# Order of the last expert stages, order of the ring's loads, and the output in parts, in a two-layer decoder on one core

## The reference, cut to what matters

```python
logits = (xf @ router_w).astype(jnp.float32) + router_b.astype(jnp.float32)
top_logit, top_e = lax.top_k(logits, TOP_K)
top_w = jax.nn.softmax(top_logit, axis=-1)
...
return (jax.nn.silu(xb @ wg[e]) * (xb @ wu[e])) @ wd[e]
...
x = x + g2 * f
```

## Time and profile before

| | |
|---|---|
| median of 3 executions | 1541.88 us (1541.83 to 1543.37) |
| profiled execution | 1549.82 us |
| its span, first to last instruction | 1547.9 us |
| PE busy | 1437.8 us (93%) |
| DVE, ACT busy | 473.4 us, 197.7 us |
| granted TensorE clock, mean | 0.984 |
| DMA, mean over the span | 311 GB/s |
| the expert layer | about 680 to 1548 us |

### The profile page before, as it was taken

How to read it: one execution, slowest core, us unless ns; L and a number is a source line. 1 busy time by engine, 2 the same in 40 slices (tenths; PEclk the granted TensorE clock), 3 DMA queues, 4 the chain that set the end, 5 groups by cost and what they waited for, 6 DMA issues and landing times.

```text
span 1547.9 us, 17255 instructions
## 1 busy us (share of the span) xinstructions
PE 1437.8 (93%) x6928; PEld 703.4 (45%) x6928; DVE 473.4 (31%) x949; ACT 197.7 (13%) x427; POOL 3.4 (0%) x32
## 2 busy tenths in 40 slices
PE   6899899999999999989777898999999999999897
PEld 2576655555544757653222333434234434343332
DVE  4478735345333565352100011101101221100103
ACT  1123223000003142321000000000001000000000
POOL 0000000000000000000000000000000000000000
PEclk9999889999999999979999999999999999999999
DMA  9945525886875333149999999999999999999995
GB/s 344 362 150 210 184 96 203 266 310 232 309 278 184 110 110 109 55 162 355 416 411 401 414 412 412 416 412 416 409 411 399 413 412 416 410 415 413 405 403 204
DMA packets 161218, 481.64 MB, mean 311 GB/s; under 512 B 18504, under 2 KB 36296, under 8 KB 146800
## 3 DMA queue, kind: packets, MB, share of 16 engines
q1 hardware_dynamic: 159688, 478.65, 80.4%
q10 hardware_dynamic: 1448, 1.84, 0.4%
HBM read 479.41 MB, written 1.06 MB: 310 GB/s over the span
## 4 chain that ended last, share of the span: by engine, by line
PE 74%; DMA 15%; DVE 5%; SPq 3%; ACT 1%; issue 1%; DVEq 0%; ACTq 0%
PE bank L1638 22%; PE bank L1674 13%; PE bank L1512 10%; DMA ring<-in_moe_wu 9%; PE bank L1234 6%; PE bank L1530 5%; PE bank L1476 4%; DMA ring<-in_moe_wg 3%; PE bank L1223 2%; DMA ring<-in_moe_wd 2%; DMA ring<-in_ada_w 1%; SPq L817 1%; PE bank L1577 1%; SPq L812 1%; DVE ada_acc L1776 1%; PE bank L1692 1%
## 5 line engine op out<-in xcount | busy, mean ns | idle before, releaser
L1638 PE MATMUL bank<-ring,h_T 128*32 128x512 f32 (+1 forms) x2240 | 300.9, 594 | 46.1 <-DMA ring<-in_moe_wu 36.1
L1674 PE MATMUL bank<-ring,m_qk_T 128*32 128x512 f32 (+2 forms) x1344 | 246.8, 594 | 14.8 <-DMA ring<-in_moe_wd 14.0
L1638 PEld LDWEIGHTS bank<-ring,h_T 128*32 128x32 f32 (+1 forms) x2240 | 92.1, 115 | 238.0 <-issue 236.4
L1638 PE MATMUL bank<-ring,cmp_region 128*128 128x512 f32 x448 | 196.3, 592 | 0.0
L1674 PEld LDWEIGHTS bank<-ring,m_qk_T 128*32 128x32 f32 (+2 forms) x1344 | 87.4, 127 | 169.8 <-issue 168.6
L1512 PE MATMUL bank<-ring,h_T 128*128 128x384 f32 (+1 forms) x448 | 156.8, 503 | 0.7 <-DVE m_s_region L2171 0.7
L1638 PEld LDWEIGHTS bank<-ring,cmp_region 128*128 128x128 f32 x448 | 84.0, 190 | 100.3 <-issue 100.3
L1234 PE MATMUL bank<-ring,h_T 128*128 128x512 f32 (+1 forms) x320 | 116.1, 512 | 0.8 <-ACT wide L923 0.5
L1512 PEld LDWEIGHTS bank<-ring,h_T 128*128 128x128 f32 x448 | 83.2, 190 | 61.3 <-issue 15.5
L2370 DVE SCALAR_TENSOR_TENSOR m_s_region<-m_s_region,bank 128x512 f32<-128x512 f32 x35 | 24.1, 688 | 255.8 <-PE bank L1638 255.8
L1069 ACT ACTIVATE m_qk_T<-bank 128x512 f32<-128x512 f32 x35 | 20.9, 597 | 637.0 <-PE bank L1654 636.3
(11 more groups left out here) (353 smaller groups left out, 1016.7 us busy)
## 6 DMA issues: line engine op xcount, KB each, us to landing
ring<-in_moe_wg SPq DMA_DIRECT2D x112, 1024.0 KB, 20.9
ring<-in_moe_wu SPq DMA_DIRECT2D x112, 1024.0 KB, 18.4
ring<-in_moe_wd SPq DMA_DIRECT2D x112, 1024.0 KB, 19.8
ring<-in_ada_w SPq DMA_DIRECT2D x28, 1024.0 KB, 8.8
ring<-in_ada_w SPq DMA_DIRECT2D x10, 2048.0 KB, 14.2
ring<-in_w_in SPq DMA_DIRECT2D x10, 2048.0 KB, 10.7
ring<-in_ffn_wg SPq DMA_DIRECT2D x6, 1536.0 KB, 10.5
ring<-in_ffn_wu SPq DMA_DIRECT2D x6, 1536.0 KB, 8.9
```

Source lines behind the costliest of these rows:

```text
L1638: last = mm(b[c0:c1, :], xT[st.team % 2][:, k, c0:c1], w, start=k == 0, stop=k == KC - 1)
L1674: last = mm(ps[half][c0:c1, :], hbT[:, unit, 128 * f + c0:128 * f + c1], w[:, D * (f % 2) + 512 * half:D * (f % 2) + 512 * half + 512], st ...
```

## The change

Four things. The last two stages of team 3 are put next to each other, and behind them those of team 4, so that stages 16 to 19 are (team 3, third span), (team 3, fourth), (team 4, third), (team 4, fourth). Team 3's four scatters go to stage 19's own hooks (`RETURN_IN[19]`): after the first and the second step of the gate part, after the up part, and after the down of stage 18. The known loads ahead of `order_ready` are ten: the eight of before and the first two of stage 1's gate part for expert 7. And the half slot of each load is chosen by `_assign`: load n goes where the load lies that PE uses up first of the 14 held, and waits for that one. The output is issued in four transfers of 128 rows of 2 KB, each as soon as its own addition is counted, ahead of the reading of the overflow count.

```diff
 for _teams in ((0,), (1, 2), (3, 4)):
-    for _s in range(len(SPANS)):
-        for _t in _teams:
-            STAGES.append(Stage(_t, _s, sum(st.units for st in STAGES)))
+    _order = [(_t, _s) for _s in range(len(SPANS)) for _t in _teams]
+    if _teams[-1] == len(TEAMS) - 1:
+        _order[-3:-1] = _order[-2], _order[-3]
+    for _t, _s in _order:
+        STAGES.append(Stage(_t, _s, sum(st.units for st in STAGES)))
...
-RETURN_IN = {5: 0, 12: 1, 13: 2}
+RETURN_IN = {5: 0, 12: 1, 13: 2, 19: 3}
...
+STEPS = []
+for _j in range(len(STAGES) + 1):
+    if _j < len(STAGES):
+        STEPS.append(("up", _j))
+    if _j:
+        STEPS.append(("down", _j - 1))
+EARLY = ((0, 0, 0), (0, 0, 1), (0, 1, 0), (0, 1, 1), (1, 0, 0))
...
-    for part in range(2):
-        for piece in range(STAGES[0].units):
-            add(STAGES[0], part, piece, (0,))
...
+    for s, part, piece in EARLY:
+        add(STAGES[s], part, piece, (0,))
+    for what, j in STEPS:
+        for part in (0, 1) if what == "up" else (2,):
+            for piece in range(STAGES[j].units):
+                add(STAGES[j], part, piece, STAGES[j].members)
...
+KNOWN = 2 * len(EARLY)
...
+def _assign():
+
+    turn = {}
+    for what, j in STEPS:
+        st = STAGES[j]
+        for part in (0, 1) if what == "up" else (2,):
+            for i in range(2 * st.units):
+                for m in st.members:
+                    turn[st.load[(part,) + divmod(i, 2) + (m,)]] = len(turn)
+    holds = list(range(SUB))
+    slot, nth, left = list(range(SUB)), [1] * SUB, [None] * SUB
+    for n in range(SUB, len(MOE_LOADS)):
+        s = min(range(SUB), key=lambda s: turn[holds[s]])
+        assert turn[holds[s]] < turn[n]
+        slot.append(s)
+        nth.append(nth[holds[s]] + 1)
+        left.append(MOE_LOADS[holds[s]][:4])
+        holds[s] = n
+    return slot, nth, left
...
-                    sub_used(sp, *MOE_LOADS[n - SUB][:4])
+                    sub_used(sp, *SUB_LEFT[n])
...
+            for n in range(2 * TT):
+                half, tt = divmod(n, 2)
+                sp.wait_ge(moe["added"], 4 * (len(TEAMS) - 1) + n + 1)
+                sp.dma_start(out[0, tt * 128:tt * 128 + 128, 512 * half:512 * half + 512], x[:, tt, 512 * half:512 * half + 512]).then_inc(out_saved, 16)
...
-            sp.wait_ge(x_final, 2 * TT)
-            for tt in range(TT):
-                sp.dma_start(out[0, tt * 128:tt * 128 + 128, :], x[:, tt, :]).then_inc(out_saved, 16)
-            sp.wait_ge(out_saved, 16 * TT)
...
+            sp.wait_ge(out_saved, 16 * 2 * TT)
...
-                        if st is STAGES[-1] and q:
-                            for n in range(4):
-                                moe_scatter(st.team - 1, n, (7, 2, 3, 4)[n])
...
-            for n in range(4):
-                add_team(len(TEAMS) - 2, n, (7, 2, 3, 4)[n])
```

More of the change, by code:

```diff
@@ L387, in _list_uses @@
+    for what, j in STEPS:
+        for part in (0, 1) if what == "up" else (2,):
+            for piece in range(STAGES[j].units):
+                add(STAGES[j], part, piece, STAGES[j].members)
 def _list_uses():
     n = 0
[L390 to L398, removed]
+    for what, j in STEPS:
+        st = STAGES[j]
+        for part in (0, 1) if what == "up" else (2,):
+            for i in range(2 * st.units - (part < 2)):
@@ L399, in _list_uses @@
                 n += 1
-                STAGES[j - 1].used[(2,) + divmod(i, 2)] = n
+                st.used[(part,) + divmod(i, 2)] = n
 _list_loads()
 _list_uses()
-assert len(MOE_LOADS) == 2 * LOADS * N_EXP and len(MOE_LOADS) % SUB == 0
-KNOWN = sum(_m == 0 for _st, _part, _, _, _m in MOE_LOADS if _st is STAGES[0] and _part < 2)
-assert all(_st is STAGES[0] and _m == 0 for _st, _, _, _, _m in MOE_LOADS[:KNOWN])
+assert len(MOE_LOADS) == 2 * LOADS * N_EXP
+KNOWN = 2 * len(EARLY)
+assert all(_st.team == 0 and _m == 0 for _st, _, _, _, _m in MOE_LOADS[:KNOWN])
@@ L410 @@
+SUB_OF, SUB_LOAD, SUB_LEFT = _assign()
 class Ordered:
@@ L679, in big_slot @@
         def big_slot(n):
-            return (n % SUB // 2 + 1) % RING
+            return (SUB_OF[n] // 2 + 1) % RING
         def moe_part(st, part, piece, q, m):
             n = st.load[part, piece, q, m]
-            return ring[:, big_slot(n), 2048 * (n % 2):2048 * (n % 2) + 2048]
+            return ring[:, big_slot(n), 2048 * (SUB_OF[n] % 2):2048 * (SUB_OF[n] % 2) + 2048]
         def moe_loaded(eng, st, part, piece, q):
@@ L691, in moe_loaded @@
                 n = st.load[part, piece, q, m]
-                eng.wait_ge(moe_full[n % SUB], 16 * (n // SUB + 1))
+                eng.wait_ge(moe_full[SUB_OF[n]], 16 * SUB_LOAD[n])
         def sub_used(eng, st, part, piece, q):
@@ L811, in _ @@
                     src = w[f0:f0 + 512, :].rearrange("(p f) n -> p (f n)", f=4)[:, 2048 * q:2048 * q + 2048]
-                    sp.dma_start(moe_part(st, part, piece, q, m), src).then_inc(moe_full[n % SUB], 16)
+                    sp.dma_start(moe_part(st, part, piece, q, m), src).then_inc(moe_full[SUB_OF[n]], 16)
                 else:
@@ L816, in _ @@
                     dst = moe_part(st, part, piece, q, m).rearrange("p (k n) -> p k n", n=c)
-                    sp.dma_start(dst, rows.rearrange("(k p) n -> p k n", p=128)).then_inc(moe_full[n % SUB], 16)
+                    sp.dma_start(dst, rows.rearrange("(k p) n -> p k n", p=128)).then_inc(moe_full[SUB_OF[n]], 16)
+            for n in range(2 * TT):
+                half, tt = divmod(n, 2)
+                sp.wait_ge(moe["added"], 4 * (len(TEAMS) - 1) + n + 1)
+                sp.dma_start(out[0, tt * 128:tt * 128 + 128, 512 * half:512 * half + 512], x[:, tt, 512 * half:512 * half + 512]).then_inc(out_saved, 16)
             sp.wait_ge(over_ready, 1)
@@ L828, in _ @@
                                 expert_load(3 * u + j, e, u, j, i * 3)
-            sp.wait_ge(x_final, 2 * TT)
-            for tt in range(TT):
-                sp.dma_start(out[0, tt * 128:tt * 128 + 128, :], x[:, tt, :]).then_inc(out_saved, 16)
-            sp.wait_ge(out_saved, 16 * TT)
+                sp.wait_ge(x_final, 2 * TT)
+                sp.wait_ge(out_saved, 16 * 2 * TT)
+                for tt in range(TT):
+                    sp.dma_start(out[0, tt * 128:tt * 128 + 128, :], x[:, tt, :]).then_inc(out_saved, 16)
+                sp.wait_ge(out_saved, 16 * 3 * TT)
+            sp.wait_ge(out_saved, 16 * 2 * TT)
         @block.gpsimd
@@ L1715, in beside @@
                         gather(moe, range(4, 8), BLK, banks=(7,), q=team % 2)
-            for j in range(len(STAGES) + 1):
+            for at, (what, j) in enumerate(STEPS):
+                ahead = what == "up" and j and ("down", j - 1) not in STEPS[:at]
                 def between(piece):
-                    if j and piece < STAGES[j - 1].units:
+                    if ahead and piece < STAGES[j - 1].units:
                         moe_turn(j - 1, piece)
                     beside(j, piece)
-                if j < len(STAGES):
+                if what == "up":
                     moe_up(j, 0, between)
@@ L1727, in _ @@
                     beside(j, 2)
[L1728 to L1733, removed]
+                    if not ahead:
+                        beside(j, 3)
+                    continue
+                if STEPS[at - 1] != ("up", j + 1):
+                    moe_turn(j, 0)
+                moe_down(j)
+                if STEPS[at - 1] == ("up", j + 1):
+                    beside(j + 1, 3)
             for n in range(4):
```

## The result

| | before | changed |
|---|---|---|
| median of 5 executions | 1543.37 us (1541.83 to 1550.65) | 1532.88 us (1528.74 to 1533.67) |
| ratio | | 0.9908, interval 0.9889 to 0.9927 |
| the same, repeated later | 1545.84 us (17 executions) | 1529.98 us; 0.9907 (0.9890 to 0.9924) |
| profiled execution | 1549.82 us, span 1547.9 us | 1533.67 us, span 1531.9 us |

The changed kernel is 0.9% faster, 14 us by the ratio (11 to 17). The forecast was 1526.2 us with 1521.5 to 1534.6, from a gain of 15.7 us. The measured gain lies inside the bounds of the prediction's sum (10.2 to 18.9 us). The measured time doesn't: those bounds ended at 1531.7, and 1532.88 is within the stated range only because that was stretched to 1534.6 to hold rivals A and B.

What follows compares the result with a forecast made beforehand. The prediction took the stream of expert loads at 411 GB/s as the bound, not PE. Front 8.4, last landing 4.6 and output 2.7 summed to 15.7 us off the 1541.88 us median: 1526.2 us, range 1521.5 to 1534.6.

Steps and rivals of the forecast that it cites:

- rivals A and B: A: only the tail comes, 7.3 us, 1534.6, chance 0.13. B: only the front comes, 8.4 us, 1533.5, chance 0.11.
- The bound: Expert layer: the stream of loads at 411 GB/s sets the end, with its start, its stops and work after the last landing.
- Two more known loads: Ahead of expert_order: loads 8 and 9 fall into dead time and take 5.1 us off the stream.
- the new hole: After loads 10 to 13, the next pair waits for PE's first step: 2.0 us lost.
- Halves by order of use: Hole at 705 to 725 us: 5.3 us won back, net 3.3 us, bounds 1 to 5.3.
- the front's 8.4: Start of the expert layer: 5.1 us from early loads plus 3.3 us net from slots by order of use.
- Stages swapped: Last stages: the new order doesn't interrupt the stream, 0 us, covered by 7.7 us of lead.
- Rival D: Single-team steps from down of stage 14 to down of stage 17: PE becomes the bound, 6.5 us slower, 1548.4; chance 0.05.
- Behind the last landing: PE's last step starts 0.1 us after the last landing instead of 4.7: 4.6 us gained, bounds 2.6 to 4.8.
- Output in four parts: Last addition to end of span: some 3.8 us in place of 6.5, 2.7 us gained, bounds 1.5 to 3.7.
- C: Whole stream: a deeper queue lifts 411 to 413 GB/s, 3.8 us more gain, 1522.4; chance 0.07.

Runs made afterwards that it cites:

- before_again: The kernel before, unchanged, profiled once more: 859.5 us from PE's first expert product to the end of the span.
- front_undone: The changed kernel with eight known loads and load n in half slot n modulo 14: 852.6 us from first expert product to end, ratio to before 0.9954.
- early_eight: The changed kernel with eight known loads ahead of the order instead of ten: 849.9 us from first expert product to end, ratio to before 0.9931.
- slots_in_turn: The changed kernel with load n in half slot n modulo 14, ten known loads kept: 856.6 us from first expert product to end, ratio to before 0.9985.

## Why the prediction was right, and where its sizes were off

**The bound.** Right. Where a part was taken back, the distance moved with the stream of loads or with what stands behind its last landing. 745 to 1514 us is still 410 GB/s.

**Two more known loads: 5.1 us.** Right: 4.0 with the new hole counted against them. The prediction booked that hole with the halves, at 2.0 us by its step-by-step count; it is 1.1 by subtraction and 1.0 by bytes. The gain hangs on the halves by order of use, which the prediction didn't say: with halves in turn, ten early loads lose 4.0 us against eight.

**Halves by order of use, 5.3 us gross: mis-sized, 2.7 to 3.0 measured.** This is the term that failed. The prediction took the bytes missing from the hole as the time lost. Two things stand against that. First, the hole is longer in that profile than it need be, and for nothing: there the loads behind expert_order start 8.6 us ahead of PE's first product, in `before_again` and `front_undone` 7.6 and 7.7. The same 20 us, 16.8 to 36.8 us behind the first product, in these two:

```profile
702.13:722.13 20.00, 20.00 (x188) 7.19 (x184) 3.01 (x6) 1.12 (x3) 0.00 (x0) 1.00 0.92 324
```

```profile
696.96:716.96 20.00, 20.00 (x188) 7.20 (x184) 3.01 (x6) 1.12 (x3) 0.00 (x0) 1.00 0.91 323
```

Before had 303. It is 4.3 us of bytes here and 5.3 there, and the last step starts at 844.9 and 845.0 all the same. Second, even like for like the landings move by less than the bytes. `early_eight` and `front_undone` differ by 361 and 329 GB/s in the windows of 52 us above, which is 4.0 us of the stream, and the end by 2.7 to 3.0. The DMA share isn't the measure either: 0.91 and 0.87 of 1.02 give 2.0 us. (In before's own window of 20 us, 0.87 of 1.02, it gives 3.0, from which the rival of `front_undone` had its 852.8. That it hit the end is luck, since on the profiles that are compared the share gives less.) `slots_in_turn` and the changed kernel repeat the pattern, in 72 us from 12 us ahead of the first product:

```profile
674.50:746.50 72.00, 63.80 (x532) 28.23 (x532) 20.99 (x88) 8.35 (x15) 0.00 (x0) 0.92 0.83 300
```

```profile
673.92:745.92 72.00, 68.50 (x594) 29.11 (x598) 22.09 (x92) 8.73 (x16) 0.00 (x0) 0.93 0.94 370
```

That is 12.3 us by bytes and 7.8 by share, where the end moved by 10.7. So the cost lies between the two. One reading is that engines which are behind keep working through a hole while the others idle; no view tells the 16 engines apart, and it stays open. The prediction's lower bound of 1 us, for engines that idle little, allowed for it, and the 2.7 to 3.0 less the new hole's 1.1 is inside its bounds. The prediction's 3.3 net stands against 2.7 gross less 1.1, so the front's 8.4 was 6.7 to 7.2.

**Stages swapped: 0 in the stream.** Right. The forecast had 12.1 us as the shortest issue-to-landing time in the new single-team stretch; the row of L842 from 1400 to 1480 us has 13.8:

```profile
DMA to landing us min/median/max: 13.8/18.7/23.4
```

against 13.7. Rival D needed that lead to vanish. It never came close.

**Behind the last landing: 4.6 us.** Right, 4.3 (4.1 in the last step): the step starts 0.1 us behind the landing as said, and the landing comes 0.5 us later than in the old order. The prediction called the turn and copy covered; the row shows 0.74 us of wait for ACT's copy on PE's chain, which is then 0.30 us from being the bound.

**Output in four parts: 2.7 us.** The size is right, 2.4, and the reason only in part: 1.0 is the overlap of the quarters with the additions, the rest the earlier issue and landing of any transfer that waits for `added`. In this trace four quarters, issued 0.7 us apart, land 2.6 to 3.5 us from issue, so they overlap. The Trainium skill (DMA: Bandwidth & Descriptors, section Bandwidth) has the rule to batch transfers to 1 MiB or more, and its section Anatomy of one DMA a fixed cost of 2.0 us for each. Both are given there for transfers issued from GpSimd, and SP issues these. An estimate by that cost, read in series, would have this part lose 4 us. The trace disagrees with the reading in series.

**The number.** 6.7 + 4.3 + 2.4 = 13.4 of 15.7, and 13.8 by the two kernels themselves. Rivals A and B each needed one part to fail and C a faster stream; none did. The distance from 1526.2 to 1532.88 is 6.7 us. 1.9 us of it are the missing gain (15.7 less 13.8). The other 4.8 are the level: the prediction took the median of three, 1541.88, at face value, and 17 executions later have 1545.84. The layer's start alone lies some 4 us apart between the two groups of profiles above. That the time still fell into the range is owed to its stretch for the rivals A and B, neither of which came.

## What to carry to other kernels

In a kernel bound by a stream of loads, look at three places first: dead time ahead of the stream that known data can fill, holes in it, and the work behind its last landing. Order the last consumers so that those with most bytes per PE time come last, and take other teams' work from behind them. Buffers filled ahead must be recycled in the order of their use, or one early load holds the whole queue back: here ten early loads with halves in turn were 4.0 us worse than eight. And compare profiles from the first instruction of the part that was changed, not by their spans.

## What the runs showed of the hardware

- A hole in the stream cost the landings less than its missing bytes and more than its missing DMA share: 2.7 to 3.0 us against 4.0 and 2.0 in one pair of profiles, 10.7 against 12.3 and 7.8 in another.
- The stream of 1 MiB loads ends thinly: in the last 6 us ahead of the last landing the DMA share was 0.50 before and 0.33 after, against 1.02 in the stream.
- The granted clock in 100 to 200 us was 0.89 to 0.91 in seven executions and 0.97 or 0.98 in seven, and the expert layer began at 685.4 to 688.2 us or at 680.2 to 684.4.
- The second of two equal output transfers of 512 KB landed 5.4 us from issue in both profiles of the kernel before, and 4.1 and 4.2 in two kernels that issue them ahead of the overflow branch; the cause is open.
